# Two boundaries of a 128-partition transformer kernel: a sum moved to VectorE, a mean put behind its slab, and ScalarE's opening order changed

## The reference

```python
def swiglu(x, w_gate, w_up, w_down):
    return (jax.nn.silu(x @ w_gate) * (x @ w_up)) @ w_down

h = x
h = h + 0.5 * swiglu(rmsnorm(h, ffn1_norm[l]), ffn1_w_gate[l], ffn1_w_up[l], ffn1_w_down[l])
...
mixed = (gate_a * y_a + gate_b * y_b) @ w_out[l]
h = h + rms_norm(mixed, mix_post_g[l])
u = rms_norm(h, ffn_pre_g[l])
gt, up = jnp.split(u @ w_ffn_in[l], 2, axis=-1)
h = h + rms_norm((jax.nn.silu(gt) * up) @ w_ffn_out[l], ffn_post_g[l])
```

## Time and profile before

| | |
|---|---|
| runs | 1027.87 us median of 3 (1027.75 to 1028.39) |
| the profiled execution | 1029.01 us, of which its span is 1027.3 |
| PE busy | 1018.7 us, 99% of the span |
| DVE, ACT, POOL busy | 696.9, 519.1 and 98.8 us |
| mean granted clock of PE | 0.998 |

### The profile page before, as it was taken

How to read it: one execution, slowest core, us unless ns; L and a number is a source line. 1 busy time by engine, 2 the same in 40 slices (tenths; PEclk the granted TensorE clock), 3 DMA queues, 4 the chain that set the end, 5 groups by cost and what they waited for, 6 DMA issues and landing times.

```text
span 1027.3 us, 20152 instructions
## 1 busy us (share of the span) xinstructions
PE 1018.7 (99%) x8773; PEld 1001.9 (98%) x8773; DVE 696.9 (68%) x692; ACT 519.1 (51%) x585; POOL 98.8 (10%) x92
## 2 busy tenths in 40 slices
PE   9999999999999999999999999999999999999997
PEld 9999999999999999999999989999999999999997
DVE  6765555777776875555679876697758677656563
ACT  6444444536737554444456576544545555434344
POOL 3000000300110200000012400110006320000000
PEclk9999999999999999999999999999999999999999
DMA  9656656475454655656555463334534537565541
GB/s 302 239 188 196 199 195 204 160 229 162 137 173 157 206 197 185 201 194 204 165 173 168 142 204 122 125 124 129 160 123 165 185 103 240 171 205 182 193 155 41
DMA packets 148241, 179.92 MB, mean 175 GB/s; under 512 B 3982, under 2 KB 135299, under 8 KB 148179
## 3 DMA queue, kind: packets, MB, share of 16 engines
q1 hardware_dynamic: 147504, 177.55, 53.3%
q0 software_dynamic: 400, 1.33, 0.4%
q10 hardware_dynamic: 274, 0.13, 0.1%
HBM read 177.95 MB, written 1.05 MB: 174 GB/s over the span
## 4 chain that ended last, share of the span: by engine, by line
PE 94%; DVE 2%; ACT 1%; DMA 1%; SPq 1%; issue 0%; DVEq 0%; ACTq 0%
PE ps L1562 29%; PE ps L1563 29%; PE ps L1564 29%; PE ps L1982 1%; DMA stage<-in_ffn_w_gate_dram 1%; ACT ar L372 1%; ACT w_hi L1183 1%; DVE w_lo L1359 0%; SPq L998 0%; PE ps L1928 0%; PE ps L1932 0%; PE ps L1986 0%; PE ps L2027 0%; PE ps L1956 0%; PE ps L1810 0%
## 5 line engine op out<-in xcount | busy, mean ns | idle before, releaser
L1359 DVE TENSOR_TENSOR w_lo<-stage,w_hi 128x2048 fp32r<-128x2048 f32 x164 | 379.3, 2314 | 176.5 <-ACT w_hi L1183 176.5
L1562 PE MATMUL ps<-x_hi,w_lo 128*128 128x256 f32 (+1 forms) x1480 | 415.4, 281 | 0.4 <-DVE w_lo L1359 0.4
L1564 PE MATMUL ps<-x_hi,w_hi 128*128 128x256 f32 (+1 forms) x1480 | 412.3, 279 | 0.0
L1563 PE MATMUL ps<-x_lo,w_hi 128*128 128x256 f32 (+1 forms) x1480 | 412.2, 279 | 0.0
L1183 ACT ACTIVATE w_hi<-stage 128x2048 fp32r<-128x2048 f32 x164 | 312.3, 1906 | 157.6 <-PE ps L1564 156.7
L1562 PE MATMUL ps<-a_hi,w_lo 128*128 128x256 f32 (+1 forms) x1112 | 309.1, 278 | 0.6 <-DVE ar L500 0.3
L1563 PE MATMUL ps<-a_lo,w_hi 128*128 128x256 f32 (+1 forms) x1112 | 307.7, 277 | 0.0
L1564 PE MATMUL ps<-a_hi,w_hi 128*128 128x256 f32 (+1 forms) x1112 | 307.7, 277 | 0.0
L1562 PEld LDWEIGHTS ps<-x_hi,w_lo 128*128 128x128 f32 x1480 | 278.3, 188 | 5.3 <-issue 3.9
L1564 PEld LDWEIGHTS ps<-x_hi,w_hi 128*128 128x128 f32 x1480 | 279.1, 189 | 0.0
L1563 PEld LDWEIGHTS ps<-x_lo,w_hi 128*128 128x128 f32 x1480 | 278.2, 188 | 0.1
(11 more groups left out here) (313 smaller groups left out, 822.0 us busy)
## 6 DMA issues: line engine op xcount, KB each, us to landing
stage<-in_w_in_dram SPq DMA_DIRECT2D x36, 1024.0 KB, 5.3
stage<-in_ffn_w_down_dram SPq DMA_DIRECT2D x22, 1024.0 KB, 5.0
stage<-in_w_ffn_in_dram SPq DMA_DIRECT2D x22, 1024.0 KB, 5.1
stage<-in_ffn_w_gate_dram SPq DMA_DIRECT2D x21, 1024.0 KB, 5.4
stage<-in_ffn_w_up_dram SPq DMA_DIRECT2D x21, 1024.0 KB, 5.3
stage<-in_w_ffn_out_dram SPq DMA_DIRECT2D x11, 1024.0 KB, 4.9
stage<-in_w_gate_dram SPq DMA_DIRECT2D x8, 1024.0 KB, 5.5
stage<-in_w_out_dram SPq DMA_DIRECT2D x8, 1024.0 KB, 5.2
```

The lines of the kernel that those rows point to most:

```text
L1359: nc.vector.tensor_tensor(o, i, b.bitcast(F32), ALU.subtract).then_inc(s["lo_ready"], 1)
L1562: nc.tensor.matmul(o, wl, xh, start=start, stop=False, skip_group_check=skip)
L1563: nc.tensor.matmul(o, wh, xl, start=False, stop=False, skip_group_check=skip)
L1564: return nc.tensor.matmul(o, wh, xh, start=False, stop=stop, skip_group_check=skip)
```

## The change

There are two groups of edits. At the start: ACT splits slab 3 ahead of its root, not behind the following table load; the copies of token pieces 1 and 2 go from DVE to ACT, behind the split of slab 4; DVE's small vectors move into the first feed-forward, behind the split of slab 10. At the boundary: ACT loads the root's table three slabs sooner; DVE adds chunk 6 of the squares to POOL's sum (new semaphore `msum_ready`), so that PE sums two parts, not three; `keep_busy` goes from 2 and 7 matmuls to 1 and 5; DVE makes the `a_lo` chunks of one pair before it adds the next pair to `h`; POOL sums the new squares two chunks wide, with four instructions in place of seven; and the mean comes behind the second slab (`late`).

```diff
@@ mixer2_act: for i in range(2, 43)
                     if j == 3:
-                        load_table(ACT.Sqrt)
                         for c in range(2):
...
                 if i < 42:
                     split_hi(n + i + 3)
+                if i == 39:
+                    load_table(ACT.Sqrt)
@@ mixer2_dve, its end
+            dve.wait_ge(s["ss_ready"], 5)
+            dve.wait_ge(s["msq_done"], 4)
+            nc.vector.tensor_tensor(ss[:, 0, X0:], ss[:, 0, X0:], sq[:, DC - 2, :], ALU.add).then_inc(s["msum_ready"], 1)
             inverse(8, rcol[:, 1, 0:2], rcol[:, 0, 0:2])
...
                 if b == 1:
                     input_lo(0, g, 32, (a_hi, a_lo), chunks=(1,))
+                else:
+                    input_lo(b - 1, g, 32, (a_hi, a_lo))
                 dve.wait_ge(s["mg_scaled"], b + 2)
                 nc.vector.tensor_tensor(hb, hb, v, ALU.add).then_inc(s["h_new"], 1)
-                if b > 1:
-                    input_lo(b - 1, g, 32, (a_hi, a_lo))
@@ gpsimd, its end
             pool.wait_ge(s["rstd_ready"], 8)
-            sum_squares(ssx, sq, "sq_done", 16)
+            ssw = ss[:, :, X0:]
+            pool.wait_ge(s["sq_done"], 18)
+            seq(nc.gpsimd.tensor_tensor(ssw, sq[:, 0:2, :], sq[:, 2:4, :], ALU.add))
+            for b in (2, 3):
+                pool.wait_ge(s["sq_done"], 17 + b)
+                seq(nc.gpsimd.tensor_tensor(ssw, ssw, sq[:, 2 * b:2 * b + 2, :], ALU.add))
+            nc.gpsimd.tensor_tensor(ssx, ss[:, 0, X0:], ss[:, 1, X0:], ALU.add).then_inc(s["ss_ready"], 1)
@@ scalar: ffn
-                split_hi(n + 3)
+                if f:
+                    split_hi(n + 3)
                 silu(J0)
                 split_hi(n + 4)
+                if f == 0:
+                    for b in (1, 2):
+                        nc.scalar.copy(h[:, 2 * b:2 * b + 2, :].rearrange("p c t -> p (c t)"), ps[:, 4 + b, :]).then_inc(s["h_new"], 1)
                 hidden_hi(J0, n + 1)
@@ scalar: ahead of the first feed-forward
             split_hi(2)
             load_table(ACT.Sqrt)
+            split_hi(3)
             root(1, ps[:, 7, 0:SEQ], loaded=True)
             load_table(ACT.Silu)
@@ vector: ahead of the first feed-forward
             split_lo(2)
-            for b in range(3):
-                tokens_in(b)
...
+            tokens_in(0)
@@ vector: ffn, ahead of its loop (small_vectors holds the lb, fg2 and gfp lines)
                 split_lo(n + 10)
+                if f == 0:
+                    small_vectors()
@@ tensor: ffn
-                                lambda: mean_mm(norm, ps[:, 2 + J0 % 2, 0:SEQ]).then_inc(s["mean_done"], 1))
+                                lambda: mean_mm(norm, ps[:, 2 + J0 % 2, 0:SEQ]).then_inc(s["mean_done"], 1), late=f == 2)
@@ tensor: mixer2, its end
-                pe.wait_ge(s["ss_ready"], 5)
-                pe.wait_ge(s["msq_done"], 4)
-                for j, v in enumerate((ss[:, 0, X0:], sq[:, DC - 2, :], sq[:, DC - 1, :])):
-                    if j == 2:
+                pe.wait_ge(s["msum_ready"], 1)
+                for j, v in enumerate((ss[:, 0, X0:], sq[:, DC - 1, :])):
+                    if j == 1:
                         pe.wait_ge(s["msq_done"], 5)
...
-                keep_busy(1, 2)
+                keep_busy(1, 1)
...
-                keep_busy(1, 7)
+                keep_busy(1, 5)
```

More of the change, by code:

```diff
@@ L109 @@
 y_bank gate_scaled silu_done up_scaled hidden hid_hi_done hid_lo_done evac
-hT_T hT_copied yg_done ysq_done yg_T out_copied
+hT_T hT_copied yg_done ysq_done yg_T out_copied msum_ready
 dve_chain dve_chain2 pool_chain
@@ L1516, in _, with small_vectors @@
             split_lo(2)
-            for b in range(3):
-                tokens_in(b)
[L1519 to L1527, removed]
+            tokens_in(0)
+            def small_vectors():
+                l0 = vec[:, VEC["lb_logits_2"]:VEC["lb_logits_2"] + DC]
+                l1 = vec[:, VEC["lb_logits_2"] + DC:VEC["lb_logits_2"] + 2 * DC]
+                seq(nc.vector.tensor_tensor(lb[:, 0, :], l0, l1, ALU.max))
+                seq(nc.vector.tensor_tensor(lb[:, 1, :], l0, lb[:, 0, :], ALU.subtract))
+                nc.vector.tensor_tensor(lb[:, 2, :], l1, lb[:, 0, :], ALU.subtract).then_inc(s["lb_ready"], 1)
+                nc.vector.tensor_tensor(fg2[:], vec[:, VEC["final_norm"]:VEC["final_norm"] + DC],
+                                        vec[:, VEC["final_norm"]:VEC["final_norm"] + DC], ALU.mult).then_inc(s["gfp_ready"], 1)
+                nc.vector.tensor_tensor(gfp[:], vec[:, VEC["final_norm"]:VEC["final_norm"] + DC],
+                                        vec[:, VEC["mix_pre_g_2"]:VEC["mix_pre_g_2"] + DC], ALU.mult).then_inc(s["gfp_ready"], 1)
             ffn(0, 1)
@@ L2135, in mixer2 @@
                         last = nc.tensor.matmul(ps[:, 4 + t, SEQ:SEQ + 2], v[:, P * t:P * t + P], ones[:, 0:2],
-                                                start=j == 0, stop=j == 2)
+                                                start=j == 0, stop=j == 1)
                 last.then_inc(s["mean_done"], 1)
-                keep_busy(1, 2)
+                keep_busy(1, 1)
                 pe.wait_ge(s["rstd_ready"], 8)
```

## The result

The changed kernel takes 1030.07 us (median of 20 runs, 1028.05 to 1032.73), the kernel before on the same chip 1027.91 us (20 runs, 1025.96 to 1029.34). The ratio is 1.0023 with a 95% interval of 1.0017 to 1.003: 2.2 us slower, where +0.9 had been forecast.

What follows compares the result with a forecast made beforehand. PE was taken to bound the kernel (94% of the chain that ended last). Start +1.0 and boundary -0.1 gave +0.9 us, taking the median from 1027.9 to 1028.8 us; range 1026.7 to 1029.9.

Steps and rivals of the forecast that it cites:

- The start, +1.0 forecast: Start: split of slab 3 waits for its load, root behind it; PE's first slab 3 matmul at 29.66, not 28.65.
- the landing stays: Start: nothing moved lies ahead of slab 3's load, issued at 13.56, taking 8.9 us, so it lands at 22.46.
- The copies and vectors at nothing: Start: two token copies moved to ACT and small vectors moved into the feed-forward cost nothing.
- First product 0.6 sooner: Boundary into third feed-forward: shorter filler and fewer spread instructions let PE's first product start at 834.9, not 835.51.
- A wait near 1 us at slab 3: Third feed-forward: PE reaches slab 3 at 852.3 but waits until 853.3 for w_lo, behind the mean's chain.
- the blocked case: Boundary: DVE and POOL's port lock delays slab 2, slab 3 starts at 853.7, +0.1; the free run gave -0.3.
- The boundary, -0.1 forecast: Boundary up to slab 3 of third feed-forward: -0.1 us, between free run and blocked one; bounds -0.6 and +0.6.
- Slab 3 landing early: Rival at the start: slab 3's load lands early enough, -0.5 - 0.1, 1027.3 us; chance 0.17.
- the boundary's whole gain: Rival: PE leaves both slabs 1.8 us sooner, no wait at slab 3, start -0.5; 1025.6 us; chance 0.07.
- The change does nothing: Rival at both places: other instructions keep both old waits, 1027.9 us; chance 0.07.
- Shared port: Rival at the boundary: port makes a_lo and splits late, +0.6, with the start's +1.0; 1029.5 us; chance 0.14.
- Slower: Rival: granted clock falls after PE stands idle at the start; 4 us at half rate give 1030.8; chance 0.07.

Runs made afterwards that it cites:

- eighth: Third experiment's kernel with DVE's order back, residual add ahead of the previous pair's a_lo rows; not timed, one profiled execution, slab 5 at 36.13 us.
- ninth: Third experiment's kernel with DVE's order back and POOL's sum one chunk wide again; not timed, one profiled execution, slab 5 at 35.97 us.
- second: Kernel before the change with the boundary's edits alone; 1026.95 us, ratio 0.9996 to the kernel before.
- third experiment: Changed kernel with ACT's split of slab 3 at the start back behind the root and its following table load; 1027.0 us, ratio 0.9997 to the kernel before.
- early splits: Third experiment's kernel with ACT's boundary splits of slabs 2, 3 and 4 and DVE's w_lo of slab 3 moved earlier; 1026.81 us, ratio 0.9997 to the kernel before.
- sixth experiment: Third experiment's kernel with POOL's sum of the new squares one chunk wide again; not timed, one profiled execution, slab 5 at 35.28 us.
- tenth: Third experiment's kernel with five filler matmuls between the mean and slab 2; not timed, one profiled execution, slab 5 at 35.98 us.

## Why the prediction was wrong, point by point

The direction was right, and at the start the place and the mechanism; the wait at the boundary stood in another place. Two terms of the sum were mis-sized: the start by 0.3 us, since slab 3 landed later than taken, and the boundary by 0.7, since `w_lo` of slab 2 came at its worst bound and the slabs behind it ran at a slower pace. The time was above the range by 0.2 us. In the profiled execution both terms of the sum came out at their upper bounds, which alone gives 1029.8 and would still be inside; for the rest there are two candidates, and neither is shown to be it: a landing later than in this trace, and the five executions with a lower granted clock, without which the median is 1029.87.

- **The start, +1.0 forecast, +1.3 measured.** The chain was right: from the start of the split to PE's first matmul of slab 3, 7.18 us were forecast and 7.13 measured. The step that failed is "the landing stays". The split began 13.09 us after PE's first product, against 12.75 in the forecast, since the load of slab 3 was issued 4.00 us after that product and not 3.83, and took 9.1 us and not 8.9. In the experiments' traces it took 8.8 to 9.7, and with the start's edits alone the loss was +1.56 in the trace. The 0.3 that I allowed for a landing that moves was the whole of its error, and not a bound.
- **The copies and vectors at nothing:** right, since the split held everything up; with the split back they gain 0.47 us (0.5 at most had been worked out). That limit holds for the slower pace only: in the three later traces with a start of 18.08 or 18.09, PE went at the faster pace, and the start was 0.84 less than before.
- **First product 0.6 sooner:** half of it. It came 5.29 after the old slab's last product against 5.60 before. The new add on DVE was not free: PE's token sums started 0.72 after that product, waiting for `ss`, where they started at 0.12 before and 0.6 had been forecast, and though one part shorter they ended 0.26 later, where no loss had been forecast.
- **The mean some 16.4 us after the old slab's end:** right. From the start of the last product it was 16.45 before and is 16.52 now.
- **A wait near 1 us at slab 3:** wrong in its place; this is the step that failed at the boundary. I played the shared port through for the last residual add and got `w_lo` of slab 2 at 848.0 at worst, 18.1 us after the start of the old slab's last product, and took the middle between this and a free run. It ended at 18.22, at the worst and a little beyond: the step that failed is the middle between the two, for a lateness that came in full in all three traces with these edits. What I hadn't put in is that the swapped `a_lo` rows stand ahead of the last residual add, and so ahead of ACT's split of slab 2 (the eighth and ninth experiments: 0.7 of 1.26 us). Slab 2 began at 18.37; after that PE came to slab 3 at 24.10 and found its `w_lo` ready since 23.27. That the blocked case came so near was in part luck, since port and order together made up the amount. In the kernel without swap and wide adds, the forecast wait at slab 3 is there (0.84 us).
- **The boundary, -0.1 forecast, +0.6 measured.** Slab 2 makes +0.1 of it, which was the blocked case. The other 0.5 is a thing that I had no term for: slabs 2 to 4 took 5.73, 5.65 and 5.61 us, where they took 5.44, 5.44 and 5.60 before. The same 0.6 stands in the traces of the second and third experiment, but the timing of the second does not confirm it.
- **Rivals.** Slab 3 landing early, and the boundary's whole gain, are refuted by the two waits. "The change does nothing" is refuted by the timing. "Shared port" named the boundary's size (+0.6), but by luck: its mechanism is less than half of what made slab 2 late, and slab 2 is only 0.1 of the 0.6. "Slower", the falling clock, is refuted for the profiled execution alone; for the five executions at 0.997 and 0.996 it is open. The windows of PE's two waits in the profile, granted clock after the five engines' busy times:

```profile
28.00:30.00 2.00, 0.54 (x5) 0.33 (x3) 2.00 (x1) 2.00 (x2) 0.00 (x0) 1.00 0.19 74
...
846.20:847.80 1.60, 0.43 (x2) 0.03 (x1) 1.60 (x2) 1.11 (x2) 0.00 (x0) 1.00 0.00 0
```

## What to carry to other kernels

An instruction moved ahead on an in-order engine takes its own wait with it: ask when its data lands, and who stands behind it. Here a split moved ahead of a 0.46 us root made the root, and all that needs it, wait 2.4 us for a DMA. Where a wait is removed, play every engine's queue through to the next two or three slabs, swapped rows included, and once one is found late, move its split up rather than fill the gap. When each term's bound is one observed size plus a little, let the range reach beyond the sum of the bounds.

## What the runs showed of the hardware that was not expected

**Matmuls have two main paces at the full granted clock.** Within a stretch, the starts of the 128x256 matmuls are for the most part either 0.1133 or 0.1178 us apart, 4%. A window of 40 us in the middle of the program, with the granted clock at 1.00 in both, holds before the change

```profile
320.00:360.00 40.00, 40.00 (x342) 40.00 (x342) 33.55 (x30) 21.13 (x24) 7.19 (x7) 1.00 0.56 185
```

and after it, in code that the change doesn't touch,

```profile
320.00:360.00 40.00, 39.67 (x349) 39.67 (x350) 34.79 (x31) 23.08 (x25) 7.20 (x7) 1.00 0.57 185
```

342 matmuls against 349. A stretch mostly keeps its pace until PE is interrupted by a wait or by other matmuls, but not always: in the eighth experiment the pace goes from 0.1133 to 0.1178 at 335.6 us without any idle time of PE, and in all 14 traces the first half of slab 4 of the third feed-forward goes at 0.120 and its second half at 0.1135, whatever the pace ahead of it. That is why the slow pace behind the boundary costs 0.5 us and no more. Counted over the whole trace (a matmul is slow where most of the 13 starts around it are over 0.1155 us apart), the slow stretches add up to 236 us before and 183 us after, and to between 160 and 214 us in the twelve experiments. The 54 us between before and after are worth 2 us, about as much as the two places cost, which is why the profiled span after (1027.5) is hardly longer than before (1027.3) although the medians differ by 2.2 us. How much of the spread between the runs of one kernel the pace makes was not shown; in the changed kernel a part of it goes with the granted clock.

The Trainium skill (TensorE: Matmul & The Clock Gate, "Wait — 56ns, not 53.3ns?") gives N / 2.4 GHz + 2.5 ns from start to start for a warm matmul; by that formula an estimate for 256 columns is 109 ns. Both measured paces, 113.3 and 117.8 ns, are longer.

What decides the pace stays open. In favour of the pause: after the wait of 1.25 or 1.26 us at slab 2, slabs 2 and 3 went at the slow pace in all three traces, and where the mean or the filler ran directly ahead of them with no such pause, at the fast one (the early splits and the filler). Against: the wait of 0.54 at slab 2 in the sixth experiment was followed by the fast pace, which turned slow at slab 3 behind an idle time of 0.06; the waits of 0.86 and 0.84 us at slab 3 in the eighth and ninth experiments were followed by the slow pace in one and the fast in the other, and slabs 0 and 1 of the third feed-forward went at 0.1134 in the third experiment and at 0.1179 in the tenth, with the same instructions up to there.
